# Prompt attention of a decoder step on one core: five rounds of 512 score columns for a head pair, and turned weights kept in blocks

## The reference

```python
s_c = jnp.einsum('bqkgd,bckd->bkgqc', qg, kc) * scale           # compressed keys
p_c = masked_softmax(s_c, mask_c)
...
s_s = jnp.einsum('bqkgd,bkqnpd->bkgqnp', qrg, k_sel) * scale    # selected blocks
p_s = masked_softmax(..., mask_s)
...
s_w = jnp.einsum('bqkgd,blkd->bkgql', qrg, kw) * scale          # sliding window
p_w = masked_softmax(s_w, mask_w)
o = gk[..., 0, :] * o_c + gk[..., 1, :] * o_s + gk[..., 2, :] * o_w
```

## Time and profile before

| | us |
|---|---|
| three runs, median (lowest to highest) | 1520.79 (1518.48 to 1522.76) |
| the profiled execution: its own time | 1520.4 |
| its span in the trace | 1518.7 |
| TensorE busy, of the span | 1468.6 (97%) |
| VectorE | 872.3 (57%) |
| ScalarE | 422.7 (28%) |
| GpSimd | 353.9 (23%) |

### The profile page before, as it was taken

One profiled execution on the slowest core, in us unless ns is written; L12 is line 12 of the kernel. 1 busy time (PEld: TensorE's weight loads), 2 busy tenths in 40 slices (PEclk: granted clock), 3 DMA queues, 4 the chain that ended last, 5 costly groups with the idle time before them and its releaser, 6 DMA issues. The chain is left out here.

```text
span 1518.7 us, 25820 instructions
## 1 busy us (share of the span) xinstructions
PE 1468.6 (97%) x9697; PEld 1220.3 (80%) x9697; DVE 872.3 (57%) x1926; ACT 422.7 (28%) x1076; POOL 353.9 (23%) x478
## 2 busy tenths in 40 slices
PE   8999999899898999999999999899999999999998
PEld 7878899555565888888888888688888888888888
DVE  2754343778653796565567734671485556676513
ACT  3011343788630343333300000433441111000012
POOL 0000300466561339993000018280000000000000
PEclk9999999899999999999999999999999999999999
DMA  8445471311196626464343320703121312322201
GB/s 272 117 123 144 140 234 47 106 32 53 51 334 213 203 83 225 143 217 152 109 127 125 111 90 0 305 30 119 61 106 57 112 65 102 111 84 83 84 28 57
DMA packets 142893, 184.34 MB, mean 121 GB/s; under 512 B 31298, under 2 KB 101642, under 8 KB 141746
## 3 DMA queue, kind: packets, MB, share of 16 engines
q1 hardware_dynamic: 139634, 174.31, 35.2%
q0 software_dynamic: 3136, 8.39, 1.6%
HBM read 163.42 MB, written 29.69 MB: 127 GB/s over the span
## 5 line engine op out<-in xcount | busy, mean ns | idle before, releaser
L2572 POOL TENSOR_SCALAR att_p<-att_p,att_tot,gates 128x512 f32<-128x512 f32 (+3 forms) x128 | 79.4, 631 | 62.1 <-DVE att_tot L2494 62.1
L296 PE MATMUL psum<-xT,l_w 128*128 128x260 f32 x384 | 85.3, 383 | 2.0 <-PEq L113 1.8
L953 PE MATMUL psum<-xT,l_w 128*128 128x260 f32 x384 | 85.2, 383 | 1.6 <-PEq L113 1.6
L296 PEld LDWEIGHTS psum<-xT,l_w 128*128 128x128 f32 x384 | 72.8, 190 | 13.5 <-issue 2.4
L953 PEld LDWEIGHTS psum<-xT,l_w 128*128 128x128 f32 x384 | 72.8, 190 | 12.9 <-issue 1.8
L969 PE MATMUL psum<-l_up_t,l_w_sums 128*128 128x260 f32 x336 | 78.2, 382 | 0.0
L2487 DVE CUSTOM_DVE_ANT_0 att_p<-psum,causal 128x512 f32<-128x512 f32 (+3 forms) x128 | 57.4, 486 | 27.9 <-PE psum L2333 27.8
L2145 PE MATMUL psum<-cmp_xt,cmp_w 64*128 64x256 f32 (+1 forms) x640 | 72.2, 362 | 0.3 <-DVE cmp_xt L2066 0.3
L2546 ACT ACTIVATE att_p<-att_p,att_low 128x512 f32<-128x512 f32 (+3 forms) x128 | 70.8, 556 | 4.7 <-DVE att_low L2487 4.1
L969 PEld LDWEIGHTS psum<-l_up_t,l_w_sums 128*128 128x128 f32 x336 | 63.8, 190 | 9.8
L2333 PE MATMUL psum<-att_kT,qrT 64*128 64x512 f32 (+3 forms) x256 | 54.3, 503 | 14.1 <-DVE att_low L2487 13.9
(11 more groups left out here) (584 smaller groups left out, 3179.9 us busy)
## 6 DMA issues: line engine op xcount, KB each, us to landing
l_w<-in_mlp_w SPq DMA_DIRECT2D x16, 2048.0 KB, 8.1
l_w<-in_mlp_w SPq DMA_DIRECT2D x32, 1024.0 KB, 5.1
proj_w<-in_nsa_w_in SPq DMA_DIRECT2D x4, 2048.0 KB, 10.4
cmp_raw<-in_cache_kv_cmp SPq DMA_DIRECT2D x24, 256.0 KB, 3.0
xT<-in_cache_kv_cmp SPq DMA_DIRECT2D x24, 256.0 KB, 3.0
sa_more<-in_cache_kv_sel POOLq DMA_DIRECT2D x44, 128.0 KB, 6.5
sa_more<-in_cache_kv_sel SPq DMA_DIRECT2D x34, 128.0 KB, 7.5
hT<-in_cache_kv_cmp SPq DMA_DIRECT2D x16, 256.0 KB, 3.0
```

The source lines that it names most:

```text
L296: mm = nc.tensor.matmul(ps[:, n % 8, 0:HALF], w[s][:, k, m * P:(m + 1) * P], src[:, kk, cols(h)], start=(kk == 0), stop=(kk == last))
L953: mm = nc.tensor.matmul(ps[:, n % 8, 0:HALF], w[s][:, k, m * P:(m + 1) * P], src[:, kk, cols(h)], start=(kk == 0), stop=(kk == last))
L2572: ve.tensor_scalar(pr[:, n % PR, par, 0:w], pr[:, n % PR, par, 0:w], tot[:, n % PR, par:par + 1], c.gates[:, i, gate:gate + 1], ALU.mult, ...
```

## The change

The same products, masking passes, exponentials and scalings are grouped otherwise. A head pair has five **rounds** in place of eight units, each with 512 score columns a head: (kind 0, tile 3); (0, 2) and (0, 0); (0, 1) and (1, 1); (1, 3); (1, 2) and (1, 0). In a round of two units both lie side by side in a bank, the masking, exponential and scaling are done for each, while one reciprocal and one copy an engine serve both. A round fills both turn banks. `LAG` is 3 rounds, `LAG_PV` 4, and `pr` has four buffers for five. `pT` is laid out in blocks of 128 x 128, so that a round's copy writes blocks at a fixed distance (`PLACES`, `place`, `slot`); of the four value products of a kind and head, the one for key tile 2 reads two blocks that lie 15 apart. The pieces of the compressed branch move to other turns. `units_to(n)` counts the units before round `n`, for the semaphores.

```diff
-    NU = NH // 2 * 2 * QT
-    LAG, LAG_PV = 4, 6
-    PR = 5
-    ORDER = (3, 0, 2, 1)
+    ROUNDS = (((0, 3),), ((0, 2), (0, 0)), ((0, 1), (1, 1)), ((1, 3),), ((1, 2), (1, 0)))
+    NR = len(ROUNDS)
+    NU = NH // 2 * NR
+    LAG, LAG_PV = 3, 4
+    PR = 4
+    LAST = (2, 4)
+    HEAD = 2 * NR
...
-        pT = c.buf("att_pT", [P, 2, 2, QT, SEQ], ctx=mine)
+        pT = c.buf("att_pT", [P, 2, 8 * QT, P], ctx=mine)
...
         def turned_back(n, z):
 
-            hp, kind, i = unit(n)
-            src = ps[:, turn_bank(n, z), :].rearrange("p (w j q) -> p w j q", w=2, q=HD)[:, :, 0:i + 1]
-            return pT[:, kind, :, 0:i + 1, i * P + z * HD:i * P + (z + 1) * HD], src
+            src, half = ps[:, turn_bank(n, z), :].rearrange("p (b q) -> p b q", q=HD), slice(z * HD, (z + 1) * HD)
+            if n % NR == 2:
+                dst = pT[:].rearrange("p k (b s) q -> p k s b q", s=4)[:, :, 1, 0:4, half]
+                return dst, src.rearrange("p (k b) q -> p k b q", k=2)
+            kind = ROUNDS[n % NR][0][0]
+            if n % NR in (1, 4):
+                return pT[:, kind, 0:16].rearrange("p (b s) q -> p s b q", s=2)[:, 0, :, half], src
+            return pT[:, kind].rearrange("p (b s) q -> p s b q", s=4)[:, 3, :, half], src
...
                 def scores(n):
...
-                        pe.wait_ge(lowered, 2 * n - 1)
+                        pe.wait_ge(lowered, units_to(n - 1) + units_to(n))
+                    for kind, i, at, w in units(n):
+                        for par in range(2):
+                            rows = slice(par * HD, par * HD + HD)
+                            mm = nc.tensor.matmul(ps[:, score_bank(n, par), at:at + w], c.qrT[rows, hp, i * P:(i + 1) * P],
+                                                  kT[rows, kind, hp // 2, 0:w], start=True, stop=True)
+                    mm.then_inc(scored, 1)
...
+                def weights(kind, par, j):
+
+                    at = place(par, j, j)
+                    return pT[:, kind, at:at + 16:15] if j == 2 else pT[:, kind, at:at + QT - j]
...
-                    if n % (4 * QT) == 2 * QT and n < NU:
-                        turn_c(n // (4 * QT))
+                    if n == NR:
+                        pe.wait_ge(c_masked, 2 * NKV)
+                    if n % HEAD == NR and n < NU:
+                        turn_c(n // HEAD)
                     for part in range(2):
                         m = n - LAG_PV - part
-                        if m >= 0 and m % QT == QT - 1:
+                        if m >= 0 and m % NR in LAST:
                             values(m, part)
...
                     if 1 <= n <= NU:
                         m = n - 1
-                        dve.wait_ge(exped, 2 * m + 2)
-                        nc.vector.reciprocal(tot[:, m % PR], tot[:, m % PR]).then_inc(recip, 1)
+                        dve.wait_ge(exped, 2 * units_to(n))
+                        sums = tot[:, m % PR, 0:len(units(m))]
+                        nc.vector.reciprocal(sums, sums).then_inc(recip, 1)
                     if n == 1:
                         mask_c(0)
+                    if n == 2:
                         mask_c(1)
-                    if n == 2:
                         mask_c(2)
                     if n == 3:
                         mask_c(3)
                     if n < NU:
-                        h, r = divmod(n, 4 * QT)
-                        if r == 1:
+                        h, r = divmod(n, HEAD)
+                        if r == (1 if h == 0 else 0):
                             least_c(h)
-                        if r == 2:
+                        if r == (2 if h == 0 else 1):
                             lower_c(h)
-                        if r == QT:
+                        if r == (3 if h == 0 else 2):
                             total_c(h)
-                        if r == QT + 1:
+                        if r == 3:
                             weight_c(h)
-                        if r == QT + 2:
+                        if r == 4:
                             weigh_c(h)
```

More of the change, by code:

```diff
@@ L2313, in turn_bank, with units, units_to, place @@
             return 3 + n % 2 * 2 + z
[L2315 to L2322 removed]
+        def units(n):
+            at, out = 0, []
+            for kind, i in ROUNDS[n % NR]:
+                out.append((kind, i, at, (i + 1) * P))
+                at += (i + 1) * P
+            return out
+        def units_to(n):
+            return n // NR * 2 * QT + sum(len(u) for u in ROUNDS[:n % NR])
+        PLACES = {(0, 0): 0, (1, 0): 1, (1, 1): 5, (2, 0): 2, (2, 1): 6, (2, 2): 4, (3, 0): 3, (3, 1): 7, (3, 2): 19, (3, 3): 23}
+        def place(par, i, j):
+            return 8 * par + PLACES[i, j]
+        def slot(n, kind, par, i, j):
+            if n % NR == 2:
+                return 4 * kind + (place(par, i, j) - 1) // 4
+            return place(par, i, j) // 2 if n % NR in (1, 4) else (place(par, i, j) - 3) // 4
+        def turned_back(n, z):
+            src, half = ps[:, turn_bank(n, z), :].rearrange("p (b q) -> p b q", q=HD), slice(z * HD, (z + 1) * HD)
+            if n % NR == 2:
+                dst = pT[:].rearrange("p k (b s) q -> p k s b q", s=4)[:, :, 1, 0:4, half]
[4 more added lines that the diff above has]
+            return pT[:, kind].rearrange("p (b s) q -> p s b q", s=4)[:, 3, :, half], src
+        def values_before(n):
+            return 2 * (n // NR) - (1 if n % NR < 2 else 0)
         with nc.Block() as block:
@@ L2365, in values @@
                                                   c.kv[:, j, 1 + kind, KVW + h * HD:KVW + (h + 1) * HD],
-                                                  pT[:, kind, par, j, j * P:SEQ], start=(kind == 0 and j == 0), stop=False)
+                                                  weights(kind, par, j), start=(kind == 0 and j == 0), stop=False)
                     if part == 0:
@@ L2480, in _ @@
                     if n < NU:
-                        hp, kind, i = unit(n)
-                        w = (i + 1) * P
                         dve.wait_ge(scored, n + 1)
```

97 lines of the change are left out of this document (49 added, 48 removed).

## The result

| | before | after |
|---|---|---|
| median, us (lowest to highest, runs) | 1521.26 (1518.48 to 1522.76, 4) | 1503.98 (1503.41 to 1505.15, 4) |
| profiled execution: time, span | 1520.4, 1518.7 | 1503.56, 1501.9 |
| stage, start to end of its last product | 270.86 to 413.91: 143.05 | 271.19 to 397.03: 125.84 |
| behind the stage, to the span's end | 1104.8 | 1104.9 |

The ratio is 0.9883 (95%: 0.9870 to 0.9896), 17.3 us faster. The stage lost 17.2 us, and nothing was given back behind it.

A forecast was written before the change was run, and what follows sets the result against it. TensorE was taken as the bound, with holes from waiting for VectorE's masking. Terms -10.1 (steady pairs), -4.5 (head), +1.5 (clock) and -1.1 (end) sum to -14.2 us, from 1520.8 to 1506.6, range 1501.5 to 1512.5.

The forecast's parts named there:

- Steady pairs: Six middle head pairs on TensorE: five rounds sum to 14.55 us for 16.24 a pair, 87.3 for 97.4, -10.1 us.
- the second setup: Split rounds' scores on TensorE: if the second pair of products needs no setup, 0.36 us less a head pair, 85.2.
- Head: Stage's start: VectorE's chain through the first rounds shortens the first head pair from 20.9 to 16.4 us, -4.5.
- The 1.5: Allowance in the stage's start for TensorE's clock falling again after idle stretches: +1.5 us, taken between 0 and 2.0.
- End: Last head pair's rounds and the drain of transposes and values: 23.6 us for 24.7, -1.1.
- the wait of 1.2: In the final drain, TensorE waits 1.2 us for GpSimd's last 512 columns.
- the slower rival: Copies into strided blocks become the bound: at 1.0 us more each, 16 us over, 1537; chance 0.04.
- GpSimd: Forecast: no wait with three rounds of lag. Rival: late products hold the transposes, 5.4 us over, 1512; chance 0.13.
- The thinnest cover: Slack between GpSimd's products and the transposes needing them: 0.6 us in rounds 0 and 1, up to 1.9.
- tightest place: VectorE in every other pair's round 0, with the compressed minimum: 5.2 us against 5.25 of work, just hidden.
- Given back: Rival: the sample stage waits for bytes coming at a fixed time, so an earlier start only lengthens it: 1520; chance 0.04.
- No fall of the clock: Rival: TensorE's clock doesn't fall in the head, single gaps being at most 2.5 us: 1.5 less, 1505.1; chance 0.17.

The follow-up runs named there:

- the second: The changed kernel unaltered, run and traced again on another chip: 1504.19 us, ratio 0.9879.
- the longer lag: Changed kernel with transposes four rounds behind scores, values five, a fifth weight buffer and `turn_c` a round later: 1505.97 us, ratio 0.9884.
- the values bunched: Changed kernel with both parts of a kind's values behind one round: 1518.57 us, ratio 0.9972; with ScalarE's output copy a round earlier too: 1515.51, 0.9947.
- spread over the old units: Kernel before, its eight units and lag kept, each kind's values dealt out in three or four parts: 1519.78 us, ratio 0.9983.
- The cut version: Changed kernel with each part of the values cut in two by the round's transposes, same products: 1520.91 us, ratio 0.9976.
- the order by head: Changed kernel with both score products of one head before the other's in a split round: 1505.44 us, ratio 0.9887.

## Why the prediction was right

The forecast was 1506.6 in 1501.5 to 1512.5, and 1503.98 came; -14.2 was summed, and the trace shows -17.2. The mechanism was right, and every part of the sum was a little too cautious: by 1.4 us in the steady pairs, 1.3 in the head and 0.3 at the end. The range is wider than its terms: 1506.6 - 2.1 - 1.5 is 1503.0, not 1501.5, and the measurement lies 1.0 above that lower sum.

- *Steady pairs*: -10.1 forecast, -11.5 measured (85.86 for 97.4). The waits went as worked out, and the rounds came as 2.04 (mean of 1.94 and 2.14), 3.21, 2.36, 3.20 and 3.41 for 2.04, 3.32, 2.47, 3.20 and 3.52. The 0.11 in each split round is the second setup, which doesn't exist: the lower bound of that term, 85.2, was the right one, with 0.5 on top for the first `turn_c`. In the steady pairs the step that failed is this one alone, taking a row of a separate product for a product that follows one of its own sort. A pair's 16.24 thus became 14.21: waits -1.42, transposes -0.27, scores -0.33.
- *Head*: -4.5 for VectorE's chain, +1.5 for the clock; -4.3 measured. The chain was right: against the stage's start, scores of rounds 3, 4 and 5 were put at 8.8, 12.3 and 16.4 and came at 9.1, 12.4 and 16.6. The clock fell, as the forecast said, but for 3.4 us, and VectorE's chain hid it. The 1.5 was mis-sized: in the first trace it was nothing, in the second 1.0. How long the clock stays low was luck, between nothing and 10.2 us in the seven traces whose first pair is worked like this one's. And the 20.9 that the forecast compared with held at least 1.6 us of low clock, which the gain of 4.3 got back; that isn't VectorE's chain.
- *End*: -1.1 forecast, -1.36 measured; the wait of 1.2 was 1.07.
- *Copies*: at 0.69 and 0.58 us the slower rival had no ground. *GpSimd*: no transposes waited for it in the steady part, and the longer lag gained nothing. The thinnest cover there was 0.44 us, not 0.6: a scaling that a subtraction had lengthened by 0.36 ended at 310.68 (the rows at the end), and its transposes began at 311.12. *VectorE*: its tightest place, rounds 0 and 1 with the compressed branch's minimum, stayed hidden; the scores at 307.80 waited for nothing. *Given back*: the rest of the kernel took 1104.9 us for 1104.8.
- *No fall of the clock* was the wrong rival for nearly the right size: the fall came in this trace and was free. That single gaps became shorter (1.96, 0.40 and 2.56 us) didn't keep the clock up.

The cause is tested on both sides. With the values bunched, the same rounds, with two groups fewer, lose 1.0 to 1.1 us a pair to the loop; with them spread over the old units, the cover exists in part but is bought with groups. The remainder, 0.6 us a pair, goes with six groups fewer (5 + 5 + 4 + 1 for 8 + 8 + 4 + 1), 0.1 a group; that is the rows added up, and no run changed the groups alone in this way. The cut version shows that a group has a price, 0.3 in its place; why the two prices differ stays open.

## What to carry to other kernels

Read the engine's own steps from one period of its timeline, and the loop through its partner beside them; a wait stands wherever the engine's work is shorter than the loop, and regrouping so that every round is longer takes it away. Count groups too: on TensorE a change from one sort of product to another costs 0.05 to 0.15 us here, and a second pair of products of the same sort nothing that shows. Where work was to be used as cover here, a few long rounds did better than many short ones. Look for a stretch of low clock in the kernel before, too: what it costs there can be part of the gain, as in the first pair here.

## What the runs showed of the hardware

- Two score products of 64 rows and 512 columns take 0.96 us together, where one of 128 rows and 512 columns takes 1.05 (301.60 to 302.65). In a split round the four products take 0.97 in either order. The Trainium skill (TensorE: Matmul & The Clock Gate, "Part 3: Packing small matmuls — row/col tiling") has products in different row groups overlap, but start and end in program order; by that, in the order by head the second head's 384 columns could start only when the first head's were done, and the round's scores would take 0.75 + 0.75; they took 0.97, and all records of 384 columns, the second head's too, had started by 307.15, ahead of the first head's 128 columns at 307.45, so here the trace disagrees. It looks as if each half of the rows takes its products by itself; that is a reading of one run's records, and no other experiment tested it.
- The clock at the stage's start differed from one execution to the next, with the same first wait (1.95 or 1.96 us). In the seven traces whose first pair is worked as in the change, it was low for 3.4 us in five, for 10.2 in one and not at all in one; in one of the five the fall came only at 288.9 us. The first pair took 16.64 to 16.67 us in all seven, since there VectorE's chain ends later.
- GpSimd's rows for two scalings of 512 columns (start, us, idle before):

```profile
302.66 1.52 POOL L2619 TENSOR_SCALAR att_p<-att_p,att_tot,gates 128x512 f32<-128x512 f32 x2 [1.19 <-DVE att_tot L2541]
...
308.80 1.88 POOL L2619 TENSOR_SCALAR att_p<-att_p,att_tot,gates 128x512 f32<-128x512 f32 x2 [0.71 <-DVE att_tot L2541]
```

The second ran beside a VectorE subtraction in SBUF (308.61, 0.67 us). It is the 0.36 that the earlier trace rows had for 128 columns. The amount depends on when the scaling begins and not on its size: in both rows it began 0.18 to 0.19 us behind the subtraction. A scaling of 384 columns that began 0.05 us ahead of one (282.16) took 1.20 us for 0.66, 0.53 more. No transposes waited for any of the three.
